# Attention in steps of head pairs, with the gate through other banks, in a hybrid decoder layer

## The reference

```
h = rms_norm(x)
q, k, v, u, g_a, g_p = split(h @ w_in)        # 512, 512, 512, 512, 1024, 1024
q, k = rope(head_norm(q)), rope(head_norm(k)) # 8 heads of 64
A = moba_attention(q, k, v)                   # causal, own block of 256 and the 3 best earlier blocks
B = multiscale_pool(u)                        # windows 2, 4, 8, 16, then a linear map per group
m = sigmoid(g_a) * (A @ w_up_attn) + sigmoid(g_p) * (B @ w_up_pool)
x = x + m @ w_out
x = x + relu(rms_norm(x) @ w_ff1)^2 @ w_ff2
```

## Time and profile before

| | |
|---|---|
| median of the runs | 939.15 us |
| lowest and highest | 939.0, 939.87 us |
| the profiled execution | 943.86 us |
| its span on the slowest core (core 1) | 942.5 us |
| spans of the eight cores | 933.8 to 942.5 us |
| PE busy | 907.6 us (96%) |
| ACT busy | 369.3 us (39%) |
| DVE busy | 457.1 us (48%) |
| POOL busy | 82.3 us (9%) |

### The profile page before, as it was taken

One profiled execution on the slowest core, in us unless ns is written; L12 is line 12 of the kernel. 1 busy time (PEld: TensorE's weight loads), 2 busy tenths in 40 slices (PEclk: granted clock), 3 DMA queues, 4 the chain that ended last, 5 costly groups with the idle time before them and its releaser, 6 DMA issues.

```text
span 942.5 us, 17189 instructions; the slowest of 8 cores (933.8 to 942.5 us)
## 1 busy us (share of the span) xinstructions
PE 907.6 (96%) x5724; PEld 463.8 (49%) x5724; DVE 457.1 (48%) x858; ACT 369.3 (39%) x730; POOL 82.3 (9%) x153
## 2 busy tenths in 40 slices
PE   2899998899999999999999999999999999999998
PEld 1454454667777754444444444444444444444444
DVE  2788875647333234335773444434443444444444
ACT  3677456798999852221006234031111221111220
POOL 4212212221000000100001000000000000000000
PEclk9999999999999999999999999999999999999999
DMA  7963352345443354983999506240065100001113
GB/s 185 224 159 79 63 135 46 52 53 83 71 69 59 67 88 114 205 182 81 189 150 147 89 1 84 40 57 1 0 90 71 21 1 1 1 1 67 67 67 156
DMA packets 65572, 78.11 MB, mean 83 GB/s; under 512 B 35216, under 2 KB 53904, under 8 KB 65232
## 3 DMA queue, kind: packets, MB, share of 16 engines
q0 software_dynamic: 24288, 40.28, 29.2%
q1 hardware_dynamic: 41200, 36.75, 14.7%
HBM read 98.41 MB, written 8.39 MB: 113 GB/s over the span
## 4 chain that ended last, share of the span: by engine, by line
PE 92%; DMA 4%; ACT 1%; issue 1%; DVE 1%; POOL 0%; ACTq 0%; DVEq 0%; POOLq 0%; SPq 0%
PE bank L1340 24%; PE bank L1368 23%; PE bank L1013 11%; PE bank L433 10%; PE bank L907 6%; PE bank L1250 6%; PE bank L945 3%; PE bank L1027 3%; PE bank L1032 3%; DMA raw<-x 2%; DMA raw<-w_slice 1%; DMA raw<-w_qkvu 1%; PE bank L487 1%; PE bank L520 1%; ACT raw L914 0%
## 5 line engine op out<-in xcount | busy, mean ns | idle before, releaser
L1340 PE MATMUL bank<-raw 128*128 128x512 bf16 x1024 | 228.0, 385 | 0.0
L1347 ACT ACTIVATE raw<-bank 128x512 f32<-128x512 f32 x128 | 76.4, 597 | 380.5 <-PE bank L1340 321.1
L1368 PE MATMUL bank<-raw 128*128 128x512 bf16 (+1 forms) x1032 | 223.3, 377 | 0.0
L1340 PEld LDWEIGHTS bank<-raw 128*128 128x128 bf16 x1024 | 101.2, 99 | 124.5 <-issue 15.2
L1368 PEld LDWEIGHTS bank<-raw 128*128 128x128 bf16 x1032 | 101.1, 98 | 120.3 <-issue 0.6
L1349 DVE SCALAR_TENSOR_TENSOR raw<-bank,raw 128x512 bf16<-128x512 f32 x128 | 88.5, 691 | 145.5 <-ACT raw L1347 144.8
L914 ACT ACTIVATE raw<-bank 128x512 bf16<-128x512 f32 (+1 forms) x288 | 146.1, 588 | 23.2 <-PE bank L945 17.0
L1375 DVE SCALAR_TENSOR_TENSOR raw<-bank,raw 128x512 f32<-128x512 f32 x129 | 96.3, 747 | 112.6 <-PE bank L1368 112.1
L433 PE MATMUL bank<-raw 128*128 128x512 bf16 x512 | 122.4, 389 | 9.4 <-ACT raw L372 3.8
L1013 PE MATMUL bank<-raw 128*128 128x512 bf16 x512 | 123.3, 381 | 0.8 <-DMA raw<-w_slice 0.8
L907 PE MATMUL bank<-raw 128*128 128x256 bf16 x576 | 99.0, 267 | 2.4 <-ACT raw L914 1.9
(11 more groups left out here) (91 smaller groups left out, 579.5 us busy)
## 6 DMA issues: line engine op xcount, KB each, us to landing
raw<-x SPq DMA_DIRECT2D x32, 512.0 KB, 6.5
raw<-w_ff POOLq DMA_DIRECT2D x16, 1024.0 KB, 13.8
raw<-w_slice POOLq DMA_DIRECT2D x22, 640.0 KB, 7.6
out<-raw SPq DMA_DIRECT2D x15, 512.0 KB, 2.6
raw<-w_qkvu POOLq DMA_DIRECT2D x8, 512.0 KB, 13.0
raw<-raw SPq DMA_DIRECT2D x2, 1024.0 KB, 4.8
raw<-w_out POOLq DMA_DIRECT2D x4, 512.0 KB, 13.9
raw<-c_ind POOLq DMA_DIRECT2D x4, 256.0 KB, 4.6
```

The source lines that it names most:

```text
L1340: t.group("pe", [lambda e, c=c, j=j, bk=bk: e.matmul(bank_f(bk), lhsT=ffw1[s][:, c, j * 128:(j + 1) * 128], rhs=hT[:, c, tg * 512:(tg + 1) ...
L1347: t.op("act", lambda e, bk=bk, si_=si_: e.activation(out=sqz[si_], in_=bank_f(bk), func=AF.Square), reads=hb[bk], writes=[b_sqz[si_]])
L1368: t.group("pe", [lambda e, j=j, bk=bk, i=i, c0_=c0_, c1_=c1_, n_=n_: e.matmul(bank_f(bk)[:, 0:n_], lhsT=a1T[ab][:, j, i * 128:(i + 1) * 12 ...
```

## The change

An attention step is now a pair of heads: 144 steps. Step i writes four score products into two neighbouring banks (0 and 1, or 2 and 3 in turn), one exponential reads both banks, and the masks are two, one per head. PT is three buffers of twice the size. The value products follow two steps later instead of four. All eight banks are one tensor, so that one instruction can span two of them. A switch for score products on half of the rows is in the code and off.

Bank 3 is no longer free: late bands and transposes of q take banks 6 and 7, where the last u projections go, with added planned lags. `gate_mm` goes to bank 6 and `gate_tr` to bank 7, each one step after the chunk with the tanh of that bank. U_LAG is 10, so two more u projections come before the last q. Sixteen units run in attention (N_ATT), sixteen in the merge. Chunks start at step 8.

```diff
-        U_LAG = 12
+        U_LAG = 10
-        N_ATT = 14
+        N_ATT = 16
-        NPT = 5
-        PT = [view(D0 + 16 * KB + i * KB, [128, 512], BF16) for i in range(NPT)]
+        NPT = 3
+        PT = [view(D0 + (16 + 2 * i) * KB, [128, 2, 512], BF16) for i in range(NPT)]
...
-            tpn = "mb" if late else "tp"
+            tpn = "pj" if late else "tp"
...
+                if late:
+                    u_.lag = 1.2
...
+                if late:
+                    tr_.only = gbank
+                    rp_.lag = 0.8
...
-        STEP_US = 0.85
-        for k_ in todo:
-            if k_.start > T_ATT - 4.0 and k_.name in ("band", "bev", "qtr", "qev"):
-                k_.start += 1.2
+        STEP_US = 1.9
...
-        gate_ps = bank_f(MISC)[:, 128:192].rearrange("p (h n) -> p h n", h=H)
+        gate_ps = bank_f(gbank[0])[:, 0:64].rearrange("p (h n) -> p h n", h=H)
...
-            tps = bank_bf(MISC)[:, 0:128]
+            tps = bank_bf(gbank[1])[:, 0:128]
...
-        LOOK = 4
+        steps = [(qb, pr, kp) for qb in range(NB) for pr in range(H // 2) for kp in range(qb + 1)]
+        LOOK = 2
+        ROW_TILED = False
...
         def emit_qk(si):
-            qb, h, kp = steps[si]
-            pr = h // 2
-            sb_ = st_banks[si % 3]
+            qb, pr, kp = steps[si]
+            b0 = 2 * (si % 2)
...
+                for e_ in range(2):
+                    ksel = kT2 if e_ else kT
+                    fns.append(lambda e, ...: e.matmul(
+                        bank_f(b0 + e_)[:, j * 256:j * 256 + 256 - qa],
+                        lhsT=ksel[r0:r1, pr, kt * 128:(kt + 1) * 128],
+                        rhs=qTz[r0:r1, 2 * pr + e_, q0 + qa:q0 + 256], start=True, stop=True))
...
-            t.op("act", lambda e: e.activation(out=pt[:, 0:nc_], in_=bank_f(sb_)[:, 0:nc_], func=AF.Exp, scale=0.125),
-                 reads=hb[sb_], writes=[b_PT[si % NPT]])
+            t.op("act", lambda e: e.activation(
+                out=pt[:, :, 0:nc_], in_=psum[:, b0 * 512:b0 * 512 + 1024].rearrange("p (e c) -> p e c", e=2)[:, :, 0:nc_],
+                func=AF.Exp, scale=0.125),
+                reads=hb[b0] + hb[b0 + 1], writes=[b_PT[si % NPT]])
             if kp == qb:
+                for e_ in range(2):
+                    dg = pt[:, e_, :].rearrange("p (a c) -> p a c", c=128)[:, 0:3:2, :]
+                    if si < 40 or si in gate_busy:
...
         for ui, u_ in enumerate(units):
-            e0 = first_of[2 * u_[1] + 2] + LOOK + 9
+            e0 = first_of[2 * u_[1] + 2] + LOOK + 5
...
+            if ui < 8:
+                chunks.append(("sel", 8 + ui))
...
+            if 1 <= ui < 9:
+                chunks.append(("tr", 7 + ui))
...
-        G_START = 14
+        G_START = 8
-        G_STEP = (NS + 3.5 - G_START) / len(chunks)
+        n_ch = sum(1 for e0, _ in chunks if not isinstance(e0, str))
+        G_STEP = (NS + LOOK - 0.25 - G_START) / n_ch
+            if isinstance(e0, str):
+                si_ = chunk_last
+                if e0 == "sel":
+                    chunk_at.setdefault(si_ + 1, []).append(lambda tt=tt: (gate_mm(tt), gate_sel(tt)))
+                    chunk_at.setdefault(si_ + 3, []).append(lambda tt=tt: gate_sel_b(tt))
+                    gate_busy.update(range(si_ - 1, si_ + 4))
+                else:
+                    chunk_at.setdefault(si_ + 1, []).append(lambda tt=tt: gate_tr(tt))
+                continue
```

More of the change, by code:

```diff
@@ L292, in build_nc @@
         wsl = [view(o_, [128, 2560], BF16) for o_ in slot_off]
-        banks = [es.enter_context(nc.psum_tensor("bank%d" % i, [128, 512], F32)) for i in range(8)]
+        psum = es.enter_context(nc.psum_tensor("psum", [128, 4096], F32))
         hb = [[Buf("psbank%d" % i, excl=True)] for i in range(8)]
         def bank_f(i):
-            return banks[i][:, :]
+            return psum[:, i * 512:(i + 1) * 512]
         def bank_bf(i):
-            return banks[i][:, :].bitcast(BF16)
+            return psum[:, i * 512:(i + 1) * 512].bitcast(BF16)
         t = Trk(nc, es)
@@ L843, in gate_mm @@
                     start=True, stop=True))
-            t.group("pe", fns, reads=[b_qT[tt], b_kmean], writes=hb[MISC])
+            t.group("pe", fns, reads=[b_qT[tt], b_kmean], writes=hb[gbank[0]])
         def gate_sel(tt):
@@ L896, in emit_qk @@
         def emit_qk(si):
-            qb, h, kp = steps[si]
-            pr = h // 2
-            sb_ = st_banks[si % 3]
+            qb, pr, kp = steps[si]
+            b0 = 2 * (si % 2)
             q0 = qb * 256
-            ksel = kT if h % 2 == 0 else kT2
+            half = ROW_TILED and (qb < 4 or kp == qb)
             fns = []
-            nc_ = 384 if kp == qb else 512
             for j in range(2):
@@ L906, in emit_qk @@
                 qa = 128 if kp == qb and j == 1 else 0
[L907 to L912, removed]
+                for e_ in range(2):
+                    ksel = kT2 if e_ else kT
+                    r0, r1 = (e_ * 64, e_ * 64 + 64) if half else (0, 128)
+                    fns.append(lambda e, kt=kt, j=j, qa=qa, e_=e_, ksel=ksel, r0=r0, r1=r1: e.matmul(
+                        bank_f(b0 + e_)[:, j * 256:j * 256 + 256 - qa],
+                        lhsT=ksel[r0:r1, pr, kt * 128:(kt + 1) * 128],
+                        rhs=qTz[r0:r1, 2 * pr + e_, q0 + qa:q0 + 256], start=True, stop=True))
@@ L928, in emit_pv @@
         def emit_pv(si):
[L929 to L932, removed]
+            qb, pr, kp = steps[si]
             pt = PT[si % NPT]
-            fns = []
-            rds = [b_PT[si % NPT], b_v[2 * kp], b_v[2 * kp + 1]]
-            for j in range(2):
-                kt = 2 * kp + j
-                for ql in range(2):
-                    if ql == 0 and kt == 2 * qb + 1:
-                        continue
-                    last = (2 * qb) if ql == 0 else (2 * qb + 1)
-                    o_ = (ql * 3 + hh) * 65
-                    dst = bank_f(bk)[:, o_:o_ + 65]
-                    c0_ = j * 256 + (0 if kt == 2 * qb + 1 else ql * 128)
-                    fns.append(lambda e, dst=dst, c0_=c0_, kt=kt, ql=ql, last=last: e.matmul(
-                        dst, lhsT=pt[:, c0_:c0_ + 128], rhs=v_aug[:, kt, h, :],
-                        start=(kt == 0 and ql == 0), stop=(kt == last), skip_group_check=True))
```

135 lines of the change are left out of this document (59 added, 76 removed).

## The result

The changed kernel takes 954.07 us (median; 953.01 to 955.79) against 939.5 before: a ratio of 1.0156, 95% interval 1.0142 to 1.017. Slower, by 14.6 us, where 1.9 were forecast; the range ended at 947.5.

The account below looks back on a forecast made before the run. PE was taken to bound the filled stretch without loss, while the entry lost 15 us to the clock, eviction waits and ACT. Entry -6.1 and selection +8.0 on 939.15 gave 941.0 us; range 934.5 to 947.5.

Parts of the forecast that it names:

- Gain 6.1: Entry into attention: full chunks begin at 186.9 instead of 193.7 us, less 0.7 for work behind; bounds 0 and 10.6.
- Steps 0 to 8: Attention's first steps, before chunks: 12.5 us, nearest to ACT's sum of 11.2; bounds 10 and 18.8.
- The steps with chunks: Entry, steps 8 to 13.3, chunks beside scores and values: 7.2 us, against 8.9 before.
- the Wp steps: Entry, eight Wp steps spanning 10.6 pairs, bound by ACT: 13.2 us, against 15.0 before.
- Two units moved: Two units moved from the merge to beside attention: 5.2 us in either place, so zero; bounds 0 and +2.
- Selection: Gate product and transpose through banks 6 and 7: 15 PE waits for the tanh at 0.53, +8.0 us; bounds 5.9 and 12.
- Pairs and bank pairs: Attention steps: pairing costs no change on PE; chunks hide the bank-pair wait; pair exponentials 1.03 us, diagonal 0.82.
- C: Rival, slower: bank pair late in the filled stretch too, some 30 steps waiting 0.3 us, +9, 950; chance 0.07.
- B: Rival, slower: pairing delays the entry, value products waiting for both heads' masks; +5.4 us, 946.5; chance 0.13.
- A: Rival, faster: entry gains all ACT allows, tanh waits at their floor; -4.7 us, 934.5; chance 0.28.
- The sum: Whole kernel: entry -6.1 plus selection +8.0 gives +1.9 us, 941.0; own range 938 to 944.

Follow-up runs that it names:

- early load: Changed kernel plus one tiny early exponential on ACT, so the table load lies before the first scores: 951.7 us, ratio 1.0133.
- two buffers: Changed kernel with attention's block output in two buffers by the parity of the query block: 953.54 us, ratio 1.0148.
- all mended: Changed kernel with selection moved, its transpose another chunk earlier, two output buffers, the tail's attention up-product deferred and a tiny early exponential: 935.88 us, ratio 0.9967.
- deferred: Changed kernel with the attention up-product of the tail's second unit placed after the third unit's gate products: 949.52 us, ratio 1.0108.
- The move alone: Changed kernel with the selection's products one step later and its transpose in the step after the attention gate's tanh: 950.31 us, ratio 1.0124.
- the part alone in the kernel before: Kernel before, with the selection of tiles 10 to 15 through banks 6 and 7, a step pair after the tanh chunk: 944.39 us, ratio 1.005.
- undoing the pair: Changed kernel with score products, exponentials, masks and value products by head, steps of pairs kept: 957.33 us; the same in all mended: 935.53 us.
- those three: Changed kernel with selection moved, two output buffers and the second tail unit's up-product deferred: 941.78 us, ratio 1.0024.
- 15 units: Changed kernel with the moved selection and 15 instead of 16 merge units beside attention: 943.82 us, ratio 1.0042.
- by head with the deferral: Products, exponentials and masks by head, up-product deferred: in the changed kernel 949.62 us, ratio 1.0089; in all mended 935.53 us, ratio 0.9969.

## Why the prediction was wrong

*The entry's "Gain 6.1": the step that failed most.* The gain came out at nothing. The first full chunk is 1.7 us earlier, but some 1.7 us more work lies behind it, where I had 0.7: six score products, 15 value products and 24 selection products more, at 0.113, 0.029 and 0.026 us from start to start.

Attention starts 2.8 us later; 3 was forecast, picked between bounds of 1.0 and 4.1, so partly by luck; U_LAG was not run alone. From there to full chunks I took 42.6 to 32.9; it was 40.9 to 36.3. On the side of before I had read the profiled core, whose clock fell twice there; cores without a fall needed 39.6. On the side of after the term that was too small is "Steps 0 to 8": 12.5 forecast, 15.7 measured. The steps with chunks took 8.5 instead of 7.2, the Wp steps 12.2 instead of 13.2.

In those steps I had summed ACT's work and let the order cost nothing. The table load, inside that sum, held PE back (36.3 to 34.6 by the early load, with a fall of the clock on four cores instead of seven). The output buffer, read until 180.6 by transposes issued at 171.82, held DVE, the selection and the value products (1.0 by two buffers). The clock fell again, on seven of eight cores: the one without needed 34.3. With all mended the four cores without a fall need 32.0, near the 32.9 forecast. So the work was counted about rightly; what failed is that waits in an order that four engines share were put at nothing.

*"Two units moved": "Zero" was wrong.* The working looked only at slices. With 14 units beside attention the tail's third unit is the first that needs the last block's output; with 16 it is the second. PE waits 2.4 to 3.2 us on each core, and the stretch is 3.0 longer (88.5 against 85.5 deferred). Where the clock falls behind the wait it is 90.5 and 90.7. The slowest core of the profiled execution is one of these two, but it also started last (156.0) and had the longest entry (38.3).

*Selection: right in place, and nearly in size.* 15 waits of 0.53 us, 8.0, were forecast, released by the tanh. From start to start PE loses 4.5 us before the eight transposes and 3.0 before the seven products of the filled stretch, the same on every core whose records are complete: 7.5, 0.50 a wait. Some 1.2 more are the copies out of bank 7, behind DVE's masks, which had no term. Moving and then mending gave 9.3 in all (167.7 to 158.4; the edits elsewhere leave that stretch at 167.5 to 168.1), of which some 0.8 isn't located. The move alone gave 6.4 because it put in new waits for the copies. That 6.4 over 15 is 0.43, the figure with which I forecast the part alone in the kernel before, is a net figure; that the part alone then cost 0.43 a wait too, behind a shorter exponential, is in part luck.

*Pairs and bank pairs: right in the filled stretch.* 1.02 and 0.82 us an exponential, no score product waits for one after the Wp steps, and undoing the pair gives 0.9 us there (0.5 with all mended). So C was wrong. B's mechanism did occur in the entry: value products wait for the pair's masks, 1.6 to 2.3 us a core, and undoing the pair takes 1.4 us off "Steps 0 to 8" (1.0 with all mended). But the entry as a whole gets only 0.1 to 0.8 us shorter, against B's 5.4, so B's sign came true mostly for other reasons. A needed an entry that this order doesn't give.

*The sum.* -1.7 at the first up-product, +9.3 selection, +3.0 seam, and the 1.7 that these two leave of the 14.0 behind it, which I put down to that work, are +12.3 in the profiled executions, 10.4 over the forecast's +1.9: 6.1 at the entry, 3.0 at the seam, 1.3 at the selection. (All mended is still 2.8 longer than before from the first up-product to the output projection: the 1.7 of work, and 1.1 in its tail, where some cores wait for slices of weights.) The median core rose by 14.1, the slowest by 15.1. What is between stays open. One part may be that the profiled execution of before had stretches at 0.81 of the clock in the feed-forward, on four cores, which no other profiled execution has; my carrying over of its difference to the median rests on that one execution. The range ended too low: the bounds that the text itself gives, 0 for the entry, 12 for the selection and 2 for the units, make 953.

## What to carry to other kernels

When work moves across a seam between stages, list for each unit behind the seam what it reads and when that lands, not its weights alone; one unit more ahead of it (the slowest core 7.7 us lower, with the selection moved), or one product deferred (5.0), gave the slowest core more than the 6.4 us that the moved selection took out of the filled stretch (3.4). A wait on a saturated in-order engine was paid in full here, so put an instruction that reuses a bank a whole chunk behind its reader, and count what reads it next. Look at all cores: where the time is that of the slowest, an edit's gain can show on the median core alone.

## What the runs showed of the hardware

In the five kernels with the wait at the seam PE stood there for 1.7 to 6.7 us on 39 of 40 profiled cores, and on 19 of them the granted clock then fell to 0.50 for 3.4 or 6.8 us. In four without it (deferred, those three, 15 units, all mended) no core of 32 waited over 0.5 us for the transposes, and none fell. The two kernels by head with the deferral lie between: four of their 16 cores waited 1.5 to 3.8 us, and the clock fell on one, the one with 3.8. Why one core falls after 2.1 us and another doesn't after 3.7 stays open.

The last two DMA transposes took 6.7 and 8.1 us from issue to landing on core 2, beside two slice loads issued at 363.88 and 367.78, and 12.5 and 13.3 on core 1 of the moved selection, whose wait was the longest; the median of the kernel's 39 is 3.9 us:
```profile
raw<-raw SPq DMA_TRANSPOSE x39, 3.9
```
